# A two-layer hybrid step: DeltaNet inverse products, bias on TensorE, convolution and conditioning moved

## The reference

```python
# neighbourhood heads (6): local window plus context, with a position bias
s_loc = q @ k_local * scale + bias            # masked outside the window
p = softmax(concat([s_loc, q @ k_ctx * scale]))
# DeltaNet heads (4, forward and backward), after a 5-tap convolution, Silu, l2norm
a_mat = strict_lower(kb @ k.T * decay)
sol = triangular_solve(I + a_mat, [v * beta, kb * exp(gc)])
# differential heads (6)
a = softmax(q1 @ k1) - lam * softmax(q2 @ k2)
o = concat(oa, rms_norm(ob) * silu(gate), rms_norm(oc) * (1 - lam_init)) @ w_out
```

## Time and profile before

| | |
|---|---|
| median of 3 runs | 3670.61 us (3667.42 to 3685.92) |
| profiled execution | 3654.36 us |
| its span, first to last instruction | 3652.6 us, granted clock 0.92 |
| busy PE / DVE / ACT / POOL | 3187.3 / 1922.4 / 1288.7 / 462.0 us |

### The profile page before, as it was taken

How to read it: one execution, slowest core, us unless ns; L and a number is a source line. 1 busy time by engine, 2 the same in 40 slices (tenths; PEclk the granted TensorE clock), 3 DMA queues, 4 the chain that set the end, 5 groups by cost and what they waited for, 6 DMA issues and landing times.

```text
span 3652.6 us, 50853 instructions
## 1 busy us (share of the span) xinstructions
PE 3187.3 (87%) x20980; PEld 2799.6 (77%) x20980; DVE 1922.4 (53%) x2967; ACT 1288.7 (35%) x1883; POOL 462.0 (13%) x443
## 2 busy tenths in 40 slices
PE   7997998899779999899979988978689898898892
PEld 5993888777679899689757886758588888788782
DVE  2214444577742222422424445776577777777776
ACT  2114111144222122121141113431466666666662
POOL 0000535000210000100024420001100000000002
PEclk9987999699889999999879986988899999999996
DMA  5243100000011122231210100002588888888783
GB/s 184 81 157 110 47 24 25 22 1 1 12 70 70 64 93 67 89 128 70 102 68 31 41 2 21 1 1 84 200 325 310 321 323 317 325 309 324 292 318 148
DMA packets 76356, 472.91 MB, mean 129 GB/s; under 512 B 10064, under 2 KB 13904, under 8 KB 26960
## 3 DMA queue, kind: packets, MB, share of 16 engines
q1 hardware_dynamic: 52512, 312.36, 23.3%
q0 software_dynamic: 23616, 157.30, 11.8%
HBM read 451.01 MB, written 27.53 MB: 131 GB/s over the span
## 4 chain that ended last, share of the span: by engine, by line
PE 68%; DVE 17%; issue 4%; ACT 4%; POOL 4%; DMA 3%; SPq 0%; ACTq 0%; DVEq 0%; POOLq 0%
PE psum L1222 11%; PE psum L1121 9%; PE psum L791 7%; PE psum L1242 5%; PE psum L814 4%; PE psum L1151 4%; PE psum L906 3%; DVE ring_rounded L1584 3%; PE psum L1082 3%; PE psum L919 3%; PE psum L1014 3%; PE psum L732 3%; DVE arena L1914 3%; PE psum L916 3%; PE psum L1029 2%
## 5 line engine op out<-in xcount | busy, mean ns | idle before, releaser
L1222 PE MATMUL psum<-stage_rounded 128*128 128x256 f32 x3488 | 584.5, 291 | 59.8 <-DVE ring_rounded L1584 38.0
L1222 PEld LDWEIGHTS psum<-stage_rounded 128*128 128x128 f32 x3488 | 511.6, 195 | 81.9 <-DVE ring_rounded L1584 51.9
L1584 DVE TENSOR_TENSOR ring_rounded<-ring,stage_rounded 128x2048 fp32r<-128x2048 f32 (+1 forms) x193 | 425.2, 2217 | 6.5 <-ACT stage_rounded L1515 6.5
L1515 ACT CAST stage_rounded<-ring 128x2048 fp32r<-128x2048 f32 (+1 forms) x193 | 358.5, 1859 | 157.2 <-DMA ring<-in_moe_gu 76.0
L1242 PE MATMUL psum<-stage_rounded 128*128 128x512 f32 x874 | 267.1, 412 | 33.1 <-DVE ring_rounded L1584 20.0
L1222 PE MATMUL psum<-ring_rounded,stage_rounded 128*128 128x256 f32 x1000 | 287.2, 287 | 0.0
L1242 PEld LDWEIGHTS psum<-stage_rounded 128*128 128x128 f32 x874 | 168.9, 195 | 81.2 <-DVE ring_rounded L1584 29.6
L1584 DVE TENSOR_TENSOR stage_rounded<-stage,stage_rounded 128x2048 fp32r<-128x2048 f32 (+1 forms) x96 | 213.0, 2227 | 4.1 <-ACT stage_rounded L1515 4.1
L1515 ACT CAST stage_rounded<-stage 128x2048 fp32r<-128x2048 f32 (+1 forms) x96 | 179.3, 1868 | 82.6 <-PE psum L1242 34.3
L1014 PE MATMUL psum<-arena,stage 128*128 128x128 f32 x1008 | 174.7, 305 | 34.9 <-DVE input L1948 20.0
L732 PE MATMUL psum<-ring,arena 128*2 128x256 f32 x768 | 174.7, 384 | 25.8 <-DMA ring<-in_ada 15.7
(11 more groups left out here) (303 smaller groups left out, 6650.3 us busy)
## 6 DMA issues: line engine op xcount, KB each, us to landing
ring<-in_moe_gu SPq DMA_DIRECT2D x63, 1024.0 KB, 6.3
ring<-in_moe_gu POOLq DMA_DIRECT2D x62, 1024.0 KB, 6.8
ring<-in_ada SPq DMA_DIRECT2D x48, 1024.0 KB, 4.8
stage<-in_moe_gu SPq DMA_DIRECT2D x31, 1024.0 KB, 6.4
stage<-in_moe_gu POOLq DMA_DIRECT2D x31, 1024.0 KB, 6.2
ring<-in_moe_down SPq DMA_DIRECT2D x28, 1024.0 KB, 6.5
ring<-in_moe_down POOLq DMA_DIRECT2D x28, 1024.0 KB, 5.7
ring<-in_unit SPq DMA_DIRECT2D x22, 1024.0 KB, 4.8
```

The costliest lines, as they stand in the source:

```text
L1222: mm = pe.matmul(bank(h % 2, 0, 2 * P), r32(x[:, cols]), w[:, k, :], start=(k == 0 and m == 0), stop=(k == KD - 1 and m == 2))
L1515: act.copy(r32(M_HIGH[q % M_HI][:, 0:n]), M_SLOT[q % M_SLOTS][:, 0:n]).then_inc(a_mhi, 1)
L1584: v.tensor_tensor(r32(w), w, high(M_HIGH[q % M_HI][:, 0:n]), ALU.subtract).then_inc(v_mlo, 1)
```

## The change

Five things are changed. *Conditioning*: the eight products of a load go to four column groups of the array (`tile_position=(0, 32 * (k % 4))`), each into 32 PSUM partitions; `scond` is spread to 32 columns a step (`spread_cond`), and the turn into columns sums the groups by `pick_cond`; the eight early loads after the rotation go, and four DeltaNet units run four loads each instead of two. *Convolution* with its Silu is interleaved with the copies of the token projection; squares and inverse norms get two buffers. *DeltaNet*: per level a lead product `A` by `XT`, a DVE multiplication that keeps only the 64 changing columns (`WH`), a transpose of `XT`, a follow product with `WH` (128 columns, the 64 repeated by a broadcast), and a DVE subtraction in place; POOL makes only the first level's mask; state products run at level 3, their right sides on DVE at levels 3 and 4. *Attention*: the bias table comes finished from the host by DMA, POOL adds the window mask a head at a time, and two products with the identity add it to the scores in PSUM; query scales are folded into the feature copies; one DVE reduction gives the negated maximum; probabilities are turned by `pe.transpose`; value products are 128 wide; na and df jobs alternate; a tile's output norm follows two and four jobs after its last job. *Experts*: eight slots instead of six, rows turned after the ninth gate/up load, `rows_low` one load later and the last `hidden_low` behind `moe_low`. The diff, cut to its core:

```diff
-M_SLOTS, M_HI = 6, 4
+M_SLOTS, M_HI = 8, 4
 M_AHEAD = M_HI - 1
+M_TURN = UF - 3
...
-ADA_EARLY = 8
+ADA_UNIT = 4
...
+        row_first = R1[:, 0:2 * 256]
+        row_second = R2[:, 2 * NLEV * P + 6 * 8 * P + TILES * 2 * W_DN:][:, 0:2 * 256]
+        scond = R2[:, 2 * NLEV * P + 6 * 8 * P + TILES * 2 * W_DN + 512:][:, 0:KD * 32]
...
+        jobs = [(0, kind, h) for kind in ("na", "df") for h in range(6)]
+        near, diff = ([(t, kind, h) for t in range(1, TILES) for h in range(6)] for kind in ("na", "df"))
+        jobs += near[:1] + [j for pair in zip(near[1:], diff) for j in pair] + diff[-1:]
+
+        NORMS = TILES + 2
+
+        tile_end = [max(n for n, j in enumerate(jobs) if j[0] == t) for t in range(TILES)]
...
                     for k in range(KD):
-                        mm = pe.matmul(bank(banks[i % 2], 0, 256)[0:2], scond[:, 2 * k:2 * k + 2], w[:, k, :],
-                                       start=(k == 0), stop=(k == KD - 1))
+                        at = 32 * (k % 4)
+                        mm = pe.matmul(bank(banks[i % 2], 0, 256)[at:at + 32],
+                                       scond[:, 32 * k:32 * k + 32], w[:, k, :],
+                                       start=(k < 4), stop=(k >= 4), tile_position=(0, at))
                     mm.then_inc(s_ada, 1)
...
-                conditioning(ADA_FIRST, ADA_FIRST + ADA_EARLY, (6, 7))
...
-                        i = ADA_FIRST + ADA_EARLY + 2 * n
-                        rows_of(i, (3, 7))
-                        rows_of(i + 1, (3, 7))
-                        columns_of(i, (3, 7))
-                        columns_of(i + 1, (3, 7))
+                        if n == 0:
+                            pe.wait_ge(s_scond, 2 * l + 2)
+                        conditioning(*ADA_BLOCKS[n + 1], (3, 7))
...
-                            mm = pe.matmul(bank(4 * d, h * P, (h + 1) * P), AS[:, d, h, :], ident, start=True, stop=True)
+                            mm = pe.transpose(bank(4 * d, h * P, (h + 1) * P), AS[:, d, h, :], ident)
...
                             for h in range(4):
-                                mm = pe.matmul(bank(4 * d, h * P, (h + 1) * P), AS[:, d, h, :], XT[:, d, h, :],
+                                mm = pe.matmul(bank(4 * d, h * P, (h + 1) * P), A[:, d, h, :], XT[:, d, h, :],
                                                start=True, stop=True)
                             mm.then_inc(s_dn[d], 1)
+                            if m > 1:
+                                if m > 2:
+                                    pe.wait_ge(a_dn[d], ab + m - 1)
+                                for h in range(4):
+                                    mm = pe.transpose(bank(4 * d + 1, h * P, (h + 1) * P), XT[:, d, h, :], ident)
+                                mm.then_inc(s_dn[d], 1)
...
-                            if m < NLEV - 1:
-                                for h in range(4):
-                                    pe.matmul(bank(4 * d + 1, h * P, (h + 1) * P), E[:, d, h, :], XX[:, d, h, :],
-                                              start=True, stop=True)
+                            else:
+                                pe.wait_ge(g_dn[d], gb + 6)
                             for h in range(4):
-                                mm = pe.matmul(bank(4 * d + 2, h * P, (h + 1) * P), XX[:, d, h, :], E[:, d, h, :],
+                                mm = pe.matmul(bank(4 * d + 2, h * P, (h + 1) * P), XX[:, d, h, :], WH[:, d, h, :].unsqueeze(1).broadcast_to([P, 2, HD]),
                                                start=True, stop=True)
                             mm.then_inc(s_dn[d], 1)
...
+                        if m == STATE_LEVEL:
...
-                for kc in range(GRID_W):
-                    g, j = kc // 5, kc % 5
-                    if g >= 2 and j == 0:
-                        pe.wait_ge(v_tab, 13 * l + g - 1)
-                    mm = pe.matmul(bank(g % 2, j * 84, (j + 1) * 84), bias_c[0:62, 63 - kc:63 - kc + P], rpbT[0:62, :],
-                                   start=True, stop=True)
-                    if j == 4 or kc == GRID_W - 1:
-                        mm.then_inc(s_tab, 1)
-
...
-                            pe.matmul(bank(b, 0, P), q, FT[rows, ki, 0:P], start=True, stop=True, tile_position=pos)
-                            mm = pe.matmul(bank(b + 1), q, FT[rows, ki, P:TOK], start=True, stop=True, tile_position=pos)
+                            pe.wait_ge(g_tab, H_NA * l + h + 1)
+                            j0 = 7 - 2 * (t - 1) - 1
+                            near_bias = tab[:, h, j0:j0 + ROWS, :].rearrange("p r k -> p (r k)")
+                            for g in range(2):
+                                pe.matmul(bank(b + g, 0, HALF), q, FT[rows, ki, g * HALF:(g + 1) * HALF],
+                                          start=True, stop=False, tile_position=pos)
+                            pe.matmul(bank(b, P, HALF), ident, near_bias[:, 0:HALF - P], start=False, stop=True)
+                            mm = pe.matmul(bank(b + 1, 0, HALF), ident, near_bias[:, HALF - P:4 * P], start=False, stop=True)
...
+                    if kind == "na":
+                        pe.wait_ge(a_exp, n_items * l + first_item[j] + 1)
+                    else:
+                        pe.wait_ge(v_p, JOBS * l + j + 1)
...
-                        mm = pe.matmul(dst, pr[:, s * P:(s + 1) * P], ident, start=True, stop=True)
+                        mm = pe.transpose(dst, pr[:, s * P:(s + 1) * P], ident)
...
-                        mm = pe.matmul(bank(7, 256, 256 + HD), probT[j % 2][:, s * P:(s + 1) * P],
-                                       VT[:, s, v_at:v_at + HD], start=(s == 0), stop=(s == n - 1))
+                        mm = pe.matmul(bank(7, 256, 256 + P), probT[j % 2][:, s * P:(s + 1) * P],
+                                       VT[:, s, v_at:v_at + P], start=(s == 0), stop=(s == n - 1))
...
+                    if f == M_TURN and i + 1 < ITEMS:
+                        turn_rows(i + 1)
...
-                    if c == 1 and i + 1 < ITEMS:
-                        turn_rows(i + 1)
...
+            def spread_cond():
+                act.activation(scond.rearrange("p (k r c) -> p k r c", k=KD, r=16),
+                               cond.rearrange("p (k c) -> p k c", k=KD).unsqueeze(2).broadcast_to([P, KD, 16, 2]),
+                               ACT.Silu).then_inc(s_scond, 1)
...
+                    if n % 4 == 3:
+                        i = n // 4
+                        act.wait_ge(v_conv, 6 * l + i + 1)
+                        act.activation(FT[:, 6 + i, :], conv_y[:, (i % 2) * TOK:(i % 2 + 1) * TOK], ACT.Silu).then_inc(a_silu, 1)
...
+                square(0)
+                for j in range(4):
+                    if j < 3:
+                        square(j + 1)
+                    inverse_norm(j)
...
-                        if p == UF + 1 and i + 1 < ITEMS:
-                            rows_low(i + 1)
...
+                        if p == UF + 2 and i + 1 < ITEMS:
+                            rows_low(i + 1)
...
+                    v.tensor_copy(VT[:, t, c * 256:c * 256 + w], bank([0, 1, 2, 3, 6, 7][n % 6], 0, w)).then_inc(v_tokm, 1)
+                    if n % 4 == 0 and n < 24:
+                        convolve(n // 4)
...
-                    for m in range(1, NLEV):
-                        for d in range(2):
-                            v.wait_ge(s_dn[d], pb + 1 + 2 * m)
-                            v.tensor_tensor(E[:, d], id4, out4(4 * d), ALU.subtract).then_inc(v_dn[d], 1)
-                        for d in range(2):
...
+                    def right_sides(d):
+                        v.wait_ge(s_dn[d], pb + dn_pe("follow", STATE_LEVEL) + 1)
...
+                    for m in range(1, NLEV):
+                        for d in range(2):
+                            v.wait_ge(s_dn[d], pb + dn_pe("lead", m))
+                            if m == 1:
+                                v.wait_ge(g_dn[d], gb + 6)
+                            v.tensor_tensor(WH[:, d].rearrange("p h (n c) -> p h n c", c=1 << m), changing4(out4(4 * d), d, m),
+                                            half_lev[:, d, m - 1].rearrange("p (n c) -> p n c", c=1 << m).unsqueeze(1)
+                                            .broadcast_to([P, 4, HD >> m, 1 << m]), ALU.mult).then_inc(v_dn[d], 1)
+                        for d in range(2):
+                            x = changing4(XT[:, d], d, m)
+                            v.wait_ge(s_dn[d], pb + dn_pe("follow", m))
+                            ins = v.tensor_tensor(x, x, out4(4 * d + 2)[:, :, 0:HD].rearrange("p h (n c) -> p h n c", c=1 << m), ALU.subtract)
+                            ins.then_inc(v_dn[d], 1)
+                        if STATE_LEVEL <= m < STATE_LEVEL + 2:
+                            right_sides(m - STATE_LEVEL)
...
-                v.wait_ge(s_bias_in, 32 * (l + 1))
-                tt3 = TT.rearrange("p (n k) -> p k n", k=GRID_W)
-                for g in range(13):
...
```

(28 more changed lines are left out.)

337 lines of the change are left out of this document (158 added, 179 removed).

## The result

The changed kernel takes 3283.8 us (median of 4 runs, 3280.9 to 3284.6) against 3669.0 for the kernel before, run beside it (4 runs, 3649.5 to 3685.9): a ratio of 0.895, 95% interval 0.891 to 0.900. It is faster, and 3283.8 lies in the range 3150 to 3345, 46 us above the 3238 forecast. The profiled execution took 3283.7 us, its span is 3282.0, against 3652.6: −370.6, where the sum said −431.

What follows compares the result with a forecast made beforehand. TensorE was taken as the main bound (68% of the chain of waits, DVE 17%). Eight terms sum to −431 us from the profiled 3654.4, giving 3223, plus 16 for the median: 3238 us, range 3150 to 3345.

Steps and rivals of the forecast that it cites:

- Conditioning, −28: Conditioning loads in four overlapping column groups: 1.2 us a load; −16 us in layer 0, −12 in layer 1.
- The serial rival: Conditioning: column groups run one after another, the −28 is lost and units grow; 3324 us, chance 0.10.
- Convolution and early conditioning, −90: Between rotation and turn of keys: convolution hidden beside token projection, early loads moved to units; −45 us a layer.
- DeltaNet units, −60: Ten units: fewer records a level, four conditioning loads free under POOL's masks; about −6 us a unit (−25 to −85).
- Bias table, −62: Bias table's stage of 32.7 us a layer goes; DMA and POOL adds replacing it are hidden (−55 to −65).
- Prompt and latent jobs, −58: Attention jobs: −6 us from the prompt's halved transpose records, −52 from latent pairs at 7.45 us, both layers.
- Output norms, −38: Before the output projection: four of five tile norms go into the jobs, about 19 us stay (−25 to −45).
- Expert items, −95: Expert stage: eight slots and earlier row turn remove both waits; items 52.6 us instead of 58.3, 17 × −5.7.
- The transfer rival: Expert stage stays bound by transfers: 56.2 us an item, −36 instead of −95; 3297 us, chance 0.22.
- The 16 us added for the median: Whole kernel: 16 us added to the sum because the median before stood that far above the profiled execution.
- own range: Whole kernel: the forecast with its terms near their size, 3190 to 3285 us, chance 0.55.
- The rule of the Trainium skill that was weighed: Levels and jobs: full clock does not engage for transposes; as a rival, they fall to 1.2 GHz, 3793 us, chance 0.03.

Runs made afterwards that it cites:

- The run with spread norms: Changed kernel with each of the four inner output norms cut into six pieces, one a job, ahead of the maxima; 3263.4 us, ratio 0.890.
- the first experiment: Changed kernel with the eight conditioning products of a load back in one column group; 3338.6 us, ratio 0.908.

## Why the prediction was right, and where it was off

The forecast's time, sign and range held; the step that failed is the one on the jobs. By its terms, both layers, measured in the profiled spans:

- **Conditioning, −28:** measured −15 (−8.9 in layer 0: the feature projection starts at 55.48, before at 64.39; −6 in layer 1). A load was put at 1.2 us and takes 1.07 in the units, but in the first block it takes 1.93 for 16 records, the pace of the load at 373.98, where the granted clock is 0.50; the input's turn runs at half its pace too until 52 us. The trace of the changed kernel has no record of the clock before 51.8 us, so there the level is read from the pace alone. The run with spread norms has it, with the same loads of 1.93; below it stands the run with one column group, with loads of 3.62:

```profile
23.60:50.80 27.20, 20.64 (x129) 14.17 (x129) 2.86 (x5) 7.33 (x21) 0.00 (x0) 0.50 0.86 320
```

```profile
21.20:58.70 37.50, 31.39 (x158) 14.46 (x157) 0.21 (x1) 6.47 (x25) 0.00 (x0) 1.00 0.59 215
```

With grouped loads five of the eight waited for their transfer, and the block ran at the lower level; that the waits are the reason is not shown apart. The serial rival is out (the first experiment).
- **Convolution and early conditioning, −90:** −88. From the start of the feature projection to the turn of keys it is −43.5 us in layer 0 and −44.9 in layer 1. The 297 that was forecast for the turn counts on the time of the kernel before; less the 8.9 us of the conditioning it is 288.1, and the turn starts at 289.70.
- **DeltaNet units, −60:** −54 (273.4 us against 302.2 in layer 0, 274.4 against 299.3 in layer 1). Units are 54.7, 54.4 and 54.7 us apart, 54.4 was forecast; a level is 4.55, 4.65 was. Two errors of the working partly cancel: levels gain a little more, and four loads were "free" only as long as they came in time. The fourth waits 2.5 to 2.9 us for its transfer, and the clock is 0.50 for some 10 us from within that wait on (below).
- **Bias table, −62:** −60. The GpSimd adds are not hidden; they cost 9 us in both layers, which count in the next term.
- **Prompt and latent jobs, −58:** +2. Here the working failed, in three places. The pair of before was taken as 211/24 = 8.8, which spreads the filling of the stage over the pairs; in its trace twelve jobs repeat after 50.48 us (744.89 to 795.37), 8.41 a pair. At a pair of 7.59 (7.45 forecast), 24 pairs give −20 a layer and not −32. The bottom-up price of the new pair was nearly right; the one of the old pair was not. The norms in the jobs were put at 7 us a layer, "DVE between jobs"; they are 20 (the norms behind the last job), some of it at a clock of 0.50. And the prompt jobs became 2 us longer instead of 3 shorter (the masks). −20 + 20 + 2 is the +1 a layer that was measured, −32 + 7 − 3 was the forecast. (By its own working the latent term is 2 × 25 = 50, not the 52 that stands there.)
- **Output norms, −38:** −37, but this is a loan: the same 20 us a layer stand in the jobs. Norms at the end give the same time.
- **Expert items, −95:** −120, items 50.67 where 52.6 was forecast and 50.5 was TensorE's bound. The transfer rival is out: the DMA moved 352 GB/s, 325 with six slots. So 352 was to be had, and what was short was the lead of the loads, together with the row turn.
- **The 16 us added for the median:** wrong as well, the profiled execution and the median agree after the change. Against 3223, the sum without it, the miss is 61 us.

The terms as measured add up to −372, and the span fell by 370.6. Their misses are +13, +2, +6, +2, +60, +1 and −25, so the jobs are the whole of the miss and the others cancel by luck: the 25 us that the experts gave beyond their term pay for the rest. Without that surplus the time would stand near 3309, outside the 3190 to 3285 that the forecast gave as its own range.

**The clock.** The rule of the Trainium skill that was weighed ("TensorE: Matmul & The Clock Gate", Part 4) is not borne out where transposes stand among products; transposes alone are shown by the earlier trace rows only. Windows of the changed kernel: two and a half levels, a dozen pairs of jobs, each with their transposes, and the stretch behind a late load.

```profile
452.80:464.20 11.40, 11.40 (x102) 11.29 (x101) 5.41 (x13) 2.93 (x5) 0.00 (x0) 1.00 0.01 1
638.90:731.00 92.10, 86.55 (x534) 63.32 (x534) 62.77 (x155) 44.01 (x95) 0.00 (x0) 1.00 0.00 1
372.70:382.90 10.20, 8.15 (x44) 6.56 (x45) 1.78 (x3) 1.09 (x5) 4.93 (x4) 0.50 0.79 309
```

Levels and jobs keep 2.4 GHz with transposes among their records; the third window begins within TensorE's wait for a transfer, from 371.1 to 373.98 us, and there the clock falls to 1.2 GHz.

**What stays open.** The run with three loads a unit gains 13.5 us; how much of it is the wait and how much the clock behind it was not separated, nor how much of the norms' 20 us a layer is clock. Why an order of jobs with the differential ones first makes the waits at a tile's end longer stays open too.

## What to carry to other kernels

Take the price of a repeated item from two starts of it in the undisturbed middle of a stage, not from the stage over its count. Work that is moved beside a full TensorE should be cut into pieces that fit the room VectorE and ScalarE have in each item, table loads included: here it cost 20 us a layer in two pieces, as much as at the end, and 9 in six. Where an engine waits for transfers, try one more buffer and the early issue together before calling the memory the bound: here the two edits alone gave 61 and 41 us, and 120 together.

## What the runs showed of the hardware

- **Column groups overlap 3.4 times over for four** (3.62 to 1.07 us for 16 records of 256 columns). The Trainium skill ("TensorE: Matmul & The Clock Gate", Part 3) measured 2.38 times for three, 0.79 of the ideal; here it is 0.85.
- **A record of 64 columns costs what one of 128 costs** in these levels: 16 take 2.01 and 2.06 us, and the level is 4.55 either way.
- **Adds on GpSimd stretch small steps of VectorE** that read two operands: from 0.22 to as much as 1.73 us for one of 128x1, from 0.35 to 1.93 for 128x128. Reciprocals and steps that read PSUM keep their time beside the adds (0.16 and 0.27 us). The Trainium skill ("GPSIMD Engine Reference", Specifications) names contention of the two engines for steps with two inputs in SBUF; the trace agrees, with up to eight times the duration.
